# Two modulated norms of a two-block transformer kernel: four-chunk groups on VectorE, factor and shift on ScalarE

## The reference

```python
mod = jax.nn.silu(c) @ w_ada[l] + b_ada[l]
shift_m, scale_m, gate_m, shift_f, scale_f, gate_f = jnp.split(mod[:, None, :], 6, axis=-1)
h = rms_norm(x, norm_mix_g[l]) * (1.0 + scale_m) + shift_m
proj = h @ w_in[l]
...
h = rms_norm(x, norm_ffn_g[l]) * (1.0 + scale_f) + shift_f
x = x + gate_f * conv_ffn(h, w_up[l], conv_ffn_w[l], conv_ffn_b[l], w_down[l])
```

## Time and profile before

| | us |
|---|---|
| median of 3 runs | 2602.12 |
| lowest, highest | 2600.09, 2602.73 |
| the profiled execution: time | 2601.97 |
| its span, first to last instruction | 2600.2 |
| TensorE busy in it | 2544.9 |
| VectorE busy | 2032.5 |
| ScalarE busy | 1325.1 |
| mean granted TensorE clock, share of full | 0.995 |

### The profile page before, as it was taken

How to read it: one execution, slowest core, us unless ns; L and a number is a source line. 1 busy time by engine, 2 the same in 40 slices (tenths; PEclk the granted TensorE clock), 3 DMA queues, 4 the chain that set the end, 5 groups by cost and what they waited for, 6 DMA issues and landing times.

```text
span 2600.2 us, 47810 instructions
## 1 busy us (share of the span) xinstructions
PE 2544.9 (98%) x14527; PEld 2207.5 (85%) x14527; DVE 2032.5 (78%) x3152; ACT 1325.1 (51%) x2048; POOL 5.2 (0%) x13
## 2 busy tenths in 40 slices
PE   8999999999999999999999999989999999999998
PEld 7888888888888888888888888868888888888886
DVE  7778775689887887887888458676888888888888
ACT  5444444565553544544554347544545545546456
POOL 0000000000000000000000000000000000000000
PEclk9999999999999999999999999999999999999999
DMA  7786874557888888888885555415455656656555
GB/s 278 264 282 202 281 238 146 181 186 267 275 283 281 280 284 274 286 283 277 281 279 187 178 179 156 141 54 187 152 186 170 201 181 179 197 178 195 190 166 158
DMA packets 160688, 561.95 MB, mean 216 GB/s; under 512 B 18131, under 2 KB 18428, under 8 KB 160636
## 3 DMA queue, kind: packets, MB, share of 16 engines
q1 hardware_dynamic: 132428, 459.04, 53.2%
q10 hardware_dynamic: 27792, 101.20, 11.9%
q0 software_dynamic: 416, 1.06, 0.3%
HBM read 559.12 MB, written 2.11 MB: 216 GB/s over the span
## 4 chain that ended last, share of the span: by engine, by line
PE 94%; DVE 3%; ACT 1%; issue 1%; DMA 1%; DVEq 0%; ACTq 0%; SPq 0%
PE bank L284 93%; DVE w_lo L993 1%; ACT w_hi L593 0%; DMA w_raw<-in_w_gate 0%; DVE R L1026 0%; PE bank L438 0%; DMA X<-in_x 0%; DVE Z L1076 0%; DVE ss L1443 0%; DVE Z L1597 0%; DVE G L1480 0%; PE bank L429 0%; DVE H L1458 0%; DVE scratch L1553 0%; DVE scratch L999 0%
## 5 line engine op out<-in xcount | busy, mean ns | idle before, releaser
L284 PE MATMUL bank<-H,w_hi 128*128 128x512 f32 (+1 forms) x4736 | 1490.7, 395 | 20.7 <-DVE w_lo L1044 9.7
L993 DVE TENSOR_TENSOR w_lo<-w_raw,w_hi 128x1024 fp32r<-128x1024 f32 x900 | 1092.1, 1222 | 144.3 <-ACT w_hi L593 136.2
L284 PEld LDWEIGHTS bank<-H,w_lo 128*128 128x128 f32 x4672 | 881.9, 189 | 203.5
L284 PE MATMUL bank<-H,w_lo 128*128 128x256 f32 x4672 | 923.9, 279 | 0.0
L593 ACT ACTIVATE w_hi<-w_raw 128x1024 fp32r<-128x1024 f32 x900 | 911.2, 1051 | 4.0 <-DMA w_raw<-in_w_gate 2.7
L284 PEld LDWEIGHTS bank<-H,w_hi 128*128 128x128 f32 x4736 | 729.8, 189 | 24.1 <-issue 11.7
L284 PE MATMUL bank<-U,w_hi 128*128 128x512 f32 x1984 | 628.0, 395 | 5.5 <-DVE U L1578 4.8
L612 ACT ACTIVATE scratch<-bank 128x256 f32<-128x256 f32 x356 | 136.6, 384 | 811.8 <-PE bank L284 811.7
L284 PEld LDWEIGHTS bank<-U,w_lo 128*128 128x128 f32 x1984 | 372.6, 188 | 86.3
L284 PE MATMUL bank<-U,w_lo 128*128 128x256 f32 x1984 | 401.7, 281 | 0.0
L284 PEld LDWEIGHTS bank<-U,w_hi 128*128 128x128 f32 x1984 | 308.3, 188 | 9.9 <-DVE U L1578 6.1
(11 more groups left out here) (200 smaller groups left out, 1183.1 us busy)
## 6 DMA issues: line engine op xcount, KB each, us to landing
w_raw<-in_w_ff SPq DMA_DIRECT2D x256, 512.0 KB, 5.1
ada_w<-in_w_ada ACTq DMA_DIRECT2D x192, 512.0 KB, 4.6
w_raw<-in_w_up SPq DMA_DIRECT2D x176, 512.0 KB, 4.0
w_raw<-in_w_z SPq DMA_DIRECT2D x96, 512.0 KB, 4.8
w_raw<-in_w_in SPq DMA_DIRECT2D x88, 512.0 KB, 3.9
w_raw<-in_w_gate SPq DMA_DIRECT2D x64, 512.0 KB, 4.4
w_raw<-in_w_down SPq DMA_DIRECT2D x64, 384.0 KB, 3.1
w_raw<-in_w_down SPq DMA_DIRECT2D x64, 320.0 KB, 3.3
```

Of the source, the lines that this page charges most:

```text
L284: return nc.tensor.matmul(out, lhsT, rhs, start=start, stop=stop, skip_group_check=True)
L993: TT(w_lo[:, slot, :], w_raw[:, slot, :], w_hi[:, slot, :].bitcast(F32), ALU.subtract)\
```

## The change

At both norms the work is divided anew. VectorE's first loop becomes six instructions, x * R alone, over groups of 1, 1, 2, 4, 4 and 4 chunks, with R repeated along the chunks. ScalarE applies gain and shift itself, in one instruction with a scale and a bias operand per partition, and does it twice for each chunk: once rounded into the high half of H (`high`), once in full, in place in Z (`full`). Its order is high 0 to 3, then high k and full k-4 in turn for k = 4 to 15, then full 12 to 15. VectorE's second loop becomes four plain subtractions over four chunks each, each behind the full values of its four chunks (`h_full`). The gains g2 are signalled by a semaphore of their own, since ScalarE now reads them.

```diff
--- before.py
+++ after.py
@@ -845,9 +845,26 @@
             for g in range(FF_GROUPS):
                 ff_group(g, g == FF_GROUPS - 1)
             root("n3", eps=1)
-            for k in range(NC):
-                act.wait_ge(sem("normed"), k + 1)
-                A(H[:, k, 0:T], zb(16 + k), ACT.Identity, bias=mod[:, k:k + 1]).then_inc(sem("h_high"), 1)
+            def modulate(gain, shift, normed):
+
+                def high(k):
+                    act.wait_ge(sem("normed"), normed + k + 1)
+                    A(H[:, k, 0:T], zb(16 + k), ACT.Identity, bias=mod[:, shift + k:shift + k + 1], scale=gain[:, k:k + 1])\
+                        .then_inc(sem("h_high"), 1)
+
+                def full(k):
+                    A(zb(16 + k), zb(16 + k), ACT.Identity, bias=mod[:, shift + k:shift + k + 1], scale=gain[:, k:k + 1])\
+                        .then_inc(sem("h_full"), 1)
+
+                for k in range(4):
+                    high(k)
+                for k in range(4, NC):
+                    high(k)
+                    full(k - 4)
+                for k in range(NC - 4, NC):
+                    full(k)
+
+            modulate(g1, 0, 0)
             root("n3b", src=bank[7])
             with act.Fori(0, 6) as i:
                 for par in range(2):
@@ -939,9 +956,8 @@
             for par in range(2):
                 gated_unit("out2", PAIR0["out2"] + 7, par, 14 + par, 14 + par, 32, True, last=par == 1)
             root("n4")
-            for k in range(NC):
-                act.wait_ge(sem("normed"), 2 * NC + k + 1)
-                A(H[:, k, 0:T], zb(16 + k), ACT.Identity, bias=mod[:, 48 + k:49 + k]).then_inc(sem("h_high"), 1)
+            act.wait_ge(sem("g2_made"), 1)
+            modulate(g2, 48, 2 * NC)
 
             def ffn_group(g, final):
                 pair = PAIR0["ffn"] + 19 * g
@@ -1337,21 +1353,21 @@
             dve.sem_inc(sem("norm.squares"), 1)
             dve.wait_ge(sem("ff.x"), FF_GROUPS * NC)
 
-            def modulated(gain, shift, chunks, normed):
-
-                for k in range(NC):
-                    STT(zb(16 + k), xb(k), gain[:, k:k + 1], R[:, :], ALU.mult, ALU.mult).then_inc(sem("normed"), 1)
-                for k in range(NC):
-                    dve.wait_ge(sem("h_high"), chunks + k + 1)
-                    dve.wait_ge(sem("normed"), normed + k + 1)
-                    STT(H[:, k, T:2 * T], zb(16 + k), mod[:, shift + k:shift + k + 1], H[:, k, 0:T].bitcast(F32),
-                        ALU.add, ALU.subtract).then_inc(sem("h_ready"), 1)
+            def modulated(nth):
+
+                for k, n in ((0, 1), (1, 1), (2, 2), (4, 4), (8, 4), (12, 4)):
+                    TT(Z[:, 16 + k:16 + k + n, :], X[:, k:k + n, :], R[:, :].unsqueeze(1).to_broadcast([P, n, T]), ALU.mult)\
+                        .then_inc(sem("normed"), n)
+                for k in range(0, NC, 4):
+                    dve.wait_ge(sem("h_full"), NC * nth + k + 4)
+                    TT(H[:, k:k + 4, T:2 * T], Z[:, 16 + k:20 + k, :], H[:, k:k + 4, 0:T].bitcast(F32), ALU.subtract)\
+                        .then_inc(sem("h_ready"), 4)
 
             inverse("n3")
-            modulated(g1, 0, CHUNKS["h3"], 0)
+            modulated(0)
             dve.wait_ge(sem("rel_made"), 1)
             v.tensor_copy(relrow[:, :], bank[6][0:8, 0:REL_W]).then_inc(sem("relrow_ready"), 1)
-            link(STT(g2[:, :], mod[:, 64:80], 1.0, V("g_ffn", 0, 16), ALU.add, ALU.mult))
+            STT(g2[:, :], mod[:, 64:80], 1.0, V("g_ffn", 0, 16), ALU.add, ALU.mult).then_inc(sem("g2_made"), 1)
 
             def plain_unit(pair, par, block):
 
@@ -1542,7 +1558,7 @@
             signal_squares("n4", "out2")
             dve.wait_ge(sem("out2.x"), NC)
             inverse("n4")
-            modulated(g2, 48, CHUNKS["h5"], 2 * NC)
+            modulated(1)
 
             def ffn_conv(pair, par, m, n):
```

## The result

| | before | changed |
|---|---|---|
| median of 6 runs, us | 2601.04 | 2612.01 |
| lowest, highest | 2598.39, 2602.73 | 2609.74, 2614.91 |
| profiled execution: time, span | 2601.97, 2600.2 | 2614.91, 2613.1 |

The changed kernel takes 1.0046 times as long (95% interval 1.0035 to 1.0056), 11.0 us more by the medians. The forecast was 11.4 us more.

A forecast was written before the change was run, and what follows sets the result against it. TensorE, busy 98% of the span, was taken as the bound, losing time where it waits at the two norms; 2 x 5.7 = 11.4 us on 2601.97, plus 0.15 for the median, gave 2613.5, range 2610.5 to 2616.5, with rivals 2606 to 2620.

The forecast's parts named there:

- ScalarE, one instruction and its step: At both norms, each ScalarE instruction with scale and bias per partition lasts 0.592 us, the next starting 0.496 us later.
- last full value: At each norm, ScalarE's last in-place instruction ends 16.50 us after VectorE's first product.
- end of the low pass: TensorE ends the low pass 19.04 us after VectorE's first product, against 13.32 before: +5.7 us per norm.
- TensorE's own work, earlier by: Without the wait for the last subtraction, TensorE's own matmuls would end the low pass only about 0.4 us earlier.
- cover of the table load at n4: ScalarE's table load and first use end about 18.1, the half copy is wanted at 19.0: 0.9 us of cover.
- pause behind it: TensorE's idleness of 2.56 us behind the low pass at both norms should stay.
- the second operand: ScalarE's second per-partition operand adds as much as the first, step 0.496 us; bounds 0.402 (free) and 0.592.
- Rival A: ScalarE's second per-partition operand is free: 2 x 3.1 = +6.2 us, 2608.3; chance 0.11.
- Rival B: TensorE's half-fed high pass lowers its clock: 1 to 4 us more per norm, 2616 to 2621; chance 0.14.
- Rival C: No loss: moved times spare all three half-clock stretches of TensorE, worth 6.9 us; chance 0.04.
- Rival D: Gain and shift cost no extra per-partition read, or in-place ScalarE instructions overlap less; step inside the bounds; chance 0.03.
- one stretch either way: TensorE's half-clock stretches move but stay as many; one such stretch, 2.7 us, more or less is forecast noise.

The follow-up runs named there:

- mixed form: Kernel before with four of sixteen chunks in the new way: their full instructions among the highs 2602.41 us (against 2598.56), behind all highs 2600.52 (against 2599.80).

## Why the prediction was right

The time forecast was 2613.5, the median measured 2612.01, with before 1.1 us lower than in its first three runs. Step by step, in us from VectorE's first product:

| step | forecast | measured at n3 |
|---|---|---|
| last of VectorE's products | 4.73 | 4.77 |
| ScalarE, one instruction and its step | 0.592, 0.496 | 0.589, 0.49 |
| last full value | 16.50 | 16.42 |
| last subtraction | 17.76 | 17.76 |
| end of the low pass | 19.04 | 19.03 |
| TensorE's own work, earlier by | about 0.4 | 0.44 (last subtraction cut) |
| cover of the table load at n4 | 0.9 | 1.1 |
| pause behind it | 2.56 | 2.56 |

The term that carried most uncertainty, the second operand, was bounded between nothing and 0.19 us of step and taken at 0.094 from the two pairs of rows; it measures 0.091 (0.589 less 0.498). The rule of the Trainium skill (ScalarE: Activation LUTs, section What ACT_TABLE_LOAD costs) gave the same, 93 ns for each; the runs with two, one and no operand (0.589, 0.498, 0.405) agree with it.

Rival A (a free second operand) is out by that row. Rival B (the half-fed high pass lowers the clock) is out: the clock was 1.00 in the pass. It did fall in the order with the highs first, but in the low pass and behind pauses of 2.55 and 0.75 us. Rival C needed three stretches at half clock to vanish; the trace shows as many, each some 6 us later, and one more. Its 6.9 us came from windows inside the stretches; the one between the norms lasts from 1672 to 1680 and not 5 us. Rival D fell with the durations: in place 0.588, into H 0.589.

What was only roughly right is the clock. The prediction counted one stretch either way as noise of 2.7 us, with no rule for where one would come. The profiled execution after has one more, behind n4, and is the slowest of its six runs. That the time still came out within 1.5 us is in part luck as far as the clock goes. With the pauses filled the two kernels differ by 11.3 us, as the ways alone would have it.

The reason for the loss in one line: VectorE's share fell from 12.8 us to 9.7, but it had been the last in line by only about 0.4 us, with TensorE's own work behind it (the low pass took 4.41 us in the kernel before and takes 4.00 where it has no wait); ScalarE's share rose from 6.5 us to 16, past both.

## What to carry to other kernels

Before moving arithmetic to an engine with idle time, lay its instructions out on the path at their step, with the price of each per-partition operand (here 0.09 us on 256 columns, more than a fifth of the plain instruction), and compare the total with what is next in line; the gain can't exceed that distance, the loss can. A total is not enough where the consumer needs the results in turn: with four of ScalarE's instructions among the highs the mixed form took 1.3 us a norm more than with four behind them. And look at the fixed pause next to the stretch that one is tuning: here two reordered instructions in it brought what the norm's arithmetic could not.

## What was not expected of the hardware

A pause of TensorE of 2.56 us is sometimes followed by a stretch at half clock and sometimes not: behind n4 the clock was 1.00 before and 0.50 after, with the same pause. The eight profiled executions whose pauses are 2.56 us long and empty (before, changed, one operand, no operand, only n3, the cut subtraction, the two mixed forms) have sixteen of them; at nine of them the clock fell to 0.50, in the pause or soon behind it. (The order with the highs first isn't counted: there the clock had fallen before the pause.) In the five executions in which the pause was filled with idle matmuls or shortened to 1.70 us or less there are ten, and behind none did it fall. The fill delayed nothing. Why it falls at one empty pause and not at the next isn't shown by these runs. The thinly fed high pass didn't lower it either: with four matmuls of 0.12 us from start to start in every 0.98 us, over 10 us, the clock stayed at 1.00.
